# The second transposition of x ahead of two norms is issued one weight unit later on TensorE

## The chip, the cores and the metric

One core of one Trainium2 chip runs the whole program in one launch. The metric is the device time of that launch in microseconds (us). All data is float32; matrix operands are split into an upper part (rounded to the format that TensorE reads in one pass) and a lower part (what is left), and every product is built from upper x upper, lower x upper and upper x lower.

## The reference, cut to what matters

The program is a stack of two transformer blocks over 256 tokens of width 1024. The part around the change is the end of the first block's mixer, its feed-forward block, and the feed-forward block that opens the second:

```
x = x + rmsnorm(mixed @ w_out, norm_mix_post)         # ends with x new, "n = 1"
h = rmsnorm(x, norm_ffn_pre)                          # norm n1
f = (silu(h @ ffn_w_gate) * (h @ ffn_w_up)) @ ffn_w_down
x = x + rmsnorm(f, norm_ffn_post)                     # x new again, "n = 2"
h = rmsnorm_2(x, ffn1_norm)                           # norm n2
x = x + 0.5 * swiglu(h, ffn1_w_gate, ffn1_w_up, ffn1_w_down)
...
k, v = split(rmsnorm_2(mem, mem_kv_norm) @ w_kv)      # norm n4, depends on the input mem alone
```

The row factor of a norm (one over the root of the mean square) is applied after the products, so the products need only x times the norm's weights, turned so that features lie on partitions.

## The kernel before

**Weights as units.** All weights stream through 358 units of up to 128 x 1024 numbers. For unit u, SyncE fetches it into one of four `raw` buffers, ScalarE makes the upper part `whi` (L1419), VectorE the lower part `wlo` (L1807), and TensorE multiplies. This pair of operations is called the split of u. A fetch of u + 4 is issued once the split of u is done; the upper part of u waits until TensorE has used u - 4.

**One order for all engines.** `order()` writes out one list of steps: "split u", "unit" (the multiplication), "end" of a product (its results leave the PSUM banks), "do" (a named piece of work) and "step" (the next piece of a spawned task). Each engine runs through the same list, in order, and issues the part that is its own. A split stands two units ahead of its multiplication (`AHEAD = 2`).

**Around the change.** There are two places.

- Place A. The product `mkv0` (a quarter of the memory's keys and values, four units 73 to 76 of 24 matmuls 128 x 256 each) does not need x. It covers the making of n1. Units 77 and 78 are the first gate/up chunk `f0gu0`, 79 and 80 the second, `f0gu1`, each unit with 8 matmuls of 512 columns and 8 of 256. Unit 77 needs features 0 to 3 (of eight groups of 128) of the turned x, unit 78 features 4 to 7.
- Place B. `mkv1` (units 143 to 146) stands in the same way ahead of n2, but is followed by `mkv2` (units 147 to 150) and `mkv3`, each unit with 12 matmuls of 512 columns. These need n4 and not x; the first gate/up unit is 155.

`new1_0` and `new1_1` are the two halves of the turning for n1, `new2_0` and `new2_1` those for n2. The list holds, for place A before the change:

```
unit 75 | split 78 | do new1_1 | unit 76 | end mkv0 | split 79 | unit 77 | step rest1 | split 80 | unit 78 | ...
```

Of `new1_1` TensorE issues eight transposes of x (L1022, `half` and `turned`) into two small PSUM banks. ScalarE issues two pairs of activations that write the upper part of the turned x with the norm's weights (L1437, L1438), and behind them the four squares with sums over x (L1459) that the norm's row factor needs. VectorE issues the four operations that write the lower part (L1822); the last of each pair says that a bank is free and the two features are ready. GpSimd and SyncE have no part in it.

Behind these stand, on ScalarE: the upper parts of 79 and 80. On VectorE: `end mkv0` (two operations, L1894, which wait for unit 76), the lower part of 79, then the first step of the task `rest1`: it adds the sums of squares (L1857), waits for two GpSimd operations (the power -0.5), polishes the root with four small operations (L1845 to L1851) and makes two diagonal matrices (L1865). Behind that stands the lower part of 80. The task's TensorE part (`across`, L1037) comes after unit 80. Place B is the same with 149 and 150 for 79 and 80, and `mkv1` for `mkv0`.

Of the kernel before, what the change touches and what calls it, by code (L numbers as in the profile page):

```python
# [310 lines left out]
def order(chunks, n_units):  # L311
# [4 lines left out]
    def split_to(u):  # L316
        while split[0] <= min(u, n_units - 1):
            yield "split", None, 0, split[0]
            split[0] += 1

    def tick():
        for name in list(left):
            yield "step", name, 0, 0
            left[name] -= 1
            n, ahead = THEN.get(name, (None, 0))
            if n and left[name] == ahead:
                spawn(n)
            if not left[name]:
                del left[name]
# [6 lines left out]
    def spawn(name):  # L336
        left[name] = STEPS[name]

    def do(name):
        yield "do", name, 0, 0  # L340

    def product(name, mid={}, end_first=False, ahead=0, open_end=False, lead=AHEAD):
        for j, u in enumerate(chunks[name]):
            yield from split_to(u + lead)
            if j in mid:
                yield from mid[j]()
            yield "unit", name, j, u
            if end_first and u == chunks[name][-1]:
                yield "end", name, 0, 0
            yield from tick()  # L350
            if u == chunks[name][-1]:
                yield from split_to(u + ahead)
        if not end_first and not open_end:
            yield "end", name, 0, 0
# [69 lines left out]
    yield from woven(("wo0", "wo1"), ahead=AHEAD + 1)  # L424
    yield from drain()
    yield from do("sum0")
    yield from product("mkv0", {2: lambda: do("new1_0"), 3: lambda: do("new1_1")})
    spawn("rest1")
    yield from ffn(0)
    yield from do("row2")  # L430
    yield from product("f0dn0", {10: drain})
    yield from product("f0dn1", ahead=AHEAD + 1)
    yield from do("sum1")
    yield from product("mkv1", {2: lambda: do("new2_0"), 3: lambda: do("new2_1")})
    spawn("rest2")
    for n in (2, 3):
        yield from product(f"mkv{n}")
# [52 lines left out]
def build(nc, io):  # L490
    with ExitStack() as ctx:
# [247 lines left out]

        units, chunks, _ = unit_plan()  # L740
        plan = list(order(chunks, len(units)))
        ends = {name: chunks[name][-1] for name in chunks}
        loaded = {u: PRODUCTS[name][0] != "a" for name in chunks for u in chunks[name]}
# [2122 lines left out]
```

## Time and profile before

| | us |
|---|---|
| median of 3 runs (1051.99 to 1052.07) | 1052.0 |
| the profiled execution's own time | 1052.19 |
| its span, first to last instruction | 1050.3 |
| TensorE (PE) busy in the span | 1040.3 |
| VectorE (DVE) busy | 773.3 |
| ScalarE (ACT) busy | 601.8 |
| GpSimd (POOL) busy | 30.7 |
| mean granted TensorE clock | 0.998 |

The profile names PE for TensorE's matmuls, PEld for its weight loads, DVE for VectorE, ACT for ScalarE, POOL for GpSimd and SPq for the queue of fetches. A matmul's duration holds its way through the array, so matmuls overlap, and the start of one to the start of the next says how long each keeps the engine. On DVE and ACT, too, an operation may start up to 0.1 us ahead of the shown end of the one before.

### The profile page before, as it was taken

How to read it: one execution, taken by the hardware profiler on the slowest of the kernel's cores; microseconds unless marked ns; L12 is line 12 of the kernel's file. 1: busy time of each engine (PE TensorE's matmuls, PEld its weight loads, DVE VectorE, ACT ScalarE, POOL GpSimd, SP SyncE). 2: the span in 40 equal slices, each digit the busy share in tenths (PEclk: the TensorE clock that was granted, in tenths of full speed). 3: DMA queues.
4: the chain of work that ended last, by engine and by line, in shares of the span. 5: the costliest groups of instructions: out<-in, count | busy, mean ns of one | idle time of the engine just before them, and what ended most of it. 6: DMA issues, size and time to landing. Idle time of an engine off the chain costs nothing.

```text
span 1050.3 us, 16507 instructions
## 1 busy us (share of the span) xinstructions
PE 1040.3 (99%) x6496; PEld 935.6 (89%) x6496; DVE 773.3 (74%) x1301; ACT 601.8 (57%) x986; POOL 30.7 (3%) x45
## 2 busy tenths in 40 slices
PE   9999999999999999999999999999999999999997
PEld 8898888899999889899898899898888999999986
DVE  5796775988888855678787555868778668888854
ACT  6653675566555644555555446546756557555653
POOL 0000500010000000000000000100000000000000
PEclk9999999999999999999999999999999999999999
DMA  8755647556666666677787568533465445666662
GB/s 287 252 176 168 200 161 250 190 180 206 196 203 203 235 193 188 213 258 217 242 284 225 172 208 316 197 120 128 136 243 182 156 142 202 199 202 199 217 197 87
DMA packets 63896, 210.91 MB, mean 201 GB/s; under 512 B 7531, under 2 KB 14883, under 8 KB 62924
## 3 DMA queue, kind: packets, MB, share of 16 engines
q1 hardware_dynamic: 63676, 209.61, 60.9%
q8 instruction: 51, 0.84, 0.3%
q10 hardware_dynamic: 144, 0.26, 0.1%
q14 instruction: 25, 0.20, 0.1%
HBM read 206.41 MB, written 5.27 MB: 202 GB/s over the span
## 4 chain that ended last, share of the span: by engine, by line
PE 93%; DVE 2%; issue 2%; ACT 1%; DMA 0%; POOL 0%; SPq 0%; POOLq 0%; DVEq 0%; ACTq 0%
PE ps L975 22%; PE ps L958 14%; PE ps L959 14%; PE ps L960 14%; PE ps L977 11%; PE ps L966 3%; PE ps L968 3%; PE ps L969 3%; PE ps L1022 1%; PE ps L1158 1%; PE ps L1144 1%; PE ps L1071 1%; PE ps L1302 1%; DVE wlo_b L1807 0%; DMA m_kvx<-m_kvs 0%
## 5 line engine op out<-in xcount | busy, mean ns | idle before, releaser
L975 PE MATMUL ps<-hT,whi_b 128*128 128x512 f32 x1056 | 346.8, 382 | 0.0
L977 PE MATMUL ps<-hT,wlo_b 128*128 128x256 f32 x1056 | 287.8, 273 | 0.0
L1807 DVE TENSOR_TENSOR wlo<-raw,whi 128x1024 fp32r<-128x1024 f32 (+1 forms) x178 | 216.4, 1228 | 79.0 <-ACT whi L1419 78.3
L1419 ACT ACTIVATE whi<-raw 128x1024 fp32r<-128x1024 f32 (+1 forms) x178 | 183.1, 1044 | 106.4 <-PE ps L960 79.2
L1807 DVE TENSOR_TENSOR wlo_b<-raw,whi_b 128x1024 fp32r<-128x1024 f32 (+2 forms) x182 | 219.4, 1210 | 25.5 <-ACT whi_b L1419 24.9
L975 PEld LDWEIGHTS ps<-hT,whi_b 128*128 128x128 f32 x1056 | 199.6, 189 | 29.0 <-issue 1.3
L1419 ACT ACTIVATE whi_b<-raw 128x1024 fp32r<-128x1024 f32 (+2 forms) x182 | 187.2, 1037 | 27.7 <-PE ps L960 12.8
L977 PEld LDWEIGHTS ps<-hT,wlo_b 128*128 128x128 f32 x1056 | 202.7, 192 | 0.0
L1508 ACT ACTIVATE f_small_part<-ps 128x512 f32<-128x512 f32 x66 | 39.6, 600 | 139.8 <-PE ps L977 139.8
L958 PE MATMUL ps<-whi,f_hid_hi 128*128 128x512 f32 x256 | 97.1, 379 | 0.0
L959 PE MATMUL ps<-wlo,f_hid_hi 128*128 128x512 f32 x256 | 97.0, 379 | 0.0
L960 PE MATMUL ps<-whi,f_hid_lo 128*128 128x512 f32 x256 | 97.0, 379 | 0.0
L958 PE MATMUL ps<-whi,hT 128*128 128x512 f32 (+1 forms) x248 | 95.4, 385 | 0.4 <-DVE wlo L1807 0.4
L959 PE MATMUL ps<-wlo,hT 128*128 128x512 f32 (+1 forms) x248 | 92.3, 372 | 0.0
L960 PE MATMUL ps<-whi,hT 128*128 128x512 f32 (+1 forms) x248 | 92.3, 372 | 0.0
L966 PE MATMUL ps<-hT,whi_b 128*128 128x256 f32 x304 | 84.9, 279 | 0.1
L969 PE MATMUL ps<-hT,whi_b 128*128 128x256 f32 x304 | 83.6, 275 | 0.0
L968 PE MATMUL ps<-hT,wlo_b 128*128 128x256 f32 x304 | 83.6, 275 | 0.0
L1987 DVE TENSOR_TENSOR f_sg<-ps,f_small_part 128x256 f32<-128x256 f32 x66 | 32.0, 484 | 58.4 <-ACT f_small_part L1508 58.4
L966 PEld LDWEIGHTS ps<-hT,whi_b 128*128 128x128 f32 x304 | 58.3, 192 | 2.4 <-issue 1.5
L968 PEld LDWEIGHTS ps<-hT,wlo_b 128*128 128x128 f32 x304 | 58.3, 192 | 0.1
L969 PEld LDWEIGHTS ps<-hT,whi_b 128*128 128x128 f32 x304 | 58.4, 192 | 0.0
(396 smaller groups left out, 1628.0 us busy)
## 6 DMA issues: line engine op xcount, KB each, us to landing
raw<-in_wflat SPq DMA_DIRECT2D x355, 512.0 KB, 4.2
wide<-scratch SPq DMA_DIRECT2D x4, 512.0 KB, 6.2
m_w<-in_cmp_k_w SPq DMA_DIRECT2D x4, 512.0 KB, 6.3
m_w<-in_cmp_v_w SPq DMA_DIRECT2D x4, 512.0 KB, 6.8
m_alibi<-in_c_alibi SPq DMA_DIRECT2D x1, 1536.0 KB, 9.3
x<-in_x SPq DMA_DIRECT2D x2, 512.0 KB, 7.3
m_memT<-in_memT SPq DMA_DIRECT2D x1, 1024.0 KB, 7.3
m_memx<-in_mem SPq DMA_DIRECT2D x1, 1024.0 KB, 9.5
```

What stands on the lines that cost most here:

```text
L958: e.matmul(o, xh, in_turn(hi[:, k, :]), start=first and k == 0, stop=False)
L959: e.matmul(o, xh, in_turn(lo[:, k, :]), start=False, stop=False)
L960: r = e.matmul(o, xl, in_turn(hi[:, k, :]), start=False, stop=last and k == kt - 1)
L966: e.matmul(o, hi[:, k, c], in_turn(xs.h(k0 + k)), start=first and k == 0 and f % 2 == 0, stop=False, skip_group_check=True)
L968: e.matmul(o, lo[:, k, c], in_turn(xs.h(k0 + k)), start=False, stop=False, skip_group_check=True)
L969: r = e.matmul(o, hi[:, k, c], in_turn(xs.l(k0 + k)), start=False, stop=last and k == kt - 1, skip_group_check=True)
L975: e.matmul(o[:, :], hi[:, k, c], xs.hl(k0 + k), start=first and k == 0, stop=False, skip_group_check=True)
L977: r = e.matmul(o[:, 0:256], lo[:, k, c], in_turn(xs.h(k0 + k)), start=False, stop=last and k == kt - 1, skip_group_check=True)
L1419: e.activation(slot(whi, u)[:, w], raw[u % NRAW][:, w], ACT.Copy).then_inc(*w_hi.did(u, c))
L1508: e.activation(small_part[:, :, :], psum[:, b:b + 2, 256:512], ACT.Copy).then_inc(*hid_s.did(i, c))
L1807: e.tensor_tensor(slot(wlo, u)[:, w], raw[u % NRAW][:, w], slot(whi, u)[:, w].bitcast(F32), ALU.subtract).then_inc(*w_lo.did(u, c))
L1987: e.tensor_tensor(o, ps.tile(name, j)[:, 0:256].rearrange("p (b a) -> p a b", a=2), small_part[:, j, :].rearrange("p (b a) -> p a b", a=2) ...
```

## The change

In both places the second half's turning is taken out of the middle of the product and put behind its last unit, ahead of the product's "end". `open_end=True` makes `product` leave out its own "end", which is written out by hand behind the moved step.

```diff
-    yield from product("mkv0", {2: lambda: do("new1_0"), 3: lambda: do("new1_1")})
+    yield from product("mkv0", {2: lambda: do("new1_0")}, open_end=True)
+    yield from do("new1_1")
+    yield "end", "mkv0", 0, 0
     spawn("rest1")
     yield from ffn(0)
...
-    yield from product("mkv1", {2: lambda: do("new2_0"), 3: lambda: do("new2_1")})
+    yield from product("mkv1", {2: lambda: do("new2_0")}, open_end=True)
+    yield from do("new2_1")
+    yield "end", "mkv1", 0, 0
     spawn("rest2")
```

The list now reads, for place A: `unit 75 | split 78 | unit 76 | do new1_1 | end mkv0 | split 79 | unit 77 | ...`.

## Rows read from the trace of the kernel before

**Rows 1.** The page: busy time and share of each engine.

```profile
PE 1040.3 (99%) x6496; PEld 935.6 (89%) x6496; DVE 773.3 (74%) x1301; ACT 601.8 (57%) x986; POOL 30.7 (3%) x45
```

**Rows 2.** Timeline of PE, place A: start, duration, engine, line, operands.

```profile
236.22 1.04 PE L1022 MATMUL ps<-cst,x 128*128 128x128 f32 x8
237.01 0.36 PE L966 MATMUL ps<-m_n_hi,whi_b 128*128 128x256 f32 x1
237.21 0.28 PE L968 MATMUL ps<-m_n_hi,wlo_b 128*128 128x256 f32 x1
...
239.78 0.38 PE L975 MATMUL ps<-hT,whi_b 128*128 128x512 f32 x1
...
242.40 0.38 PE L975 MATMUL ps<-hT,whi_b 128*128 128x512 f32 x1
...
245.02 0.38 PE L975 MATMUL ps<-hT,whi_b 128*128 128x512 f32 x1
...
247.64 0.38 PE L975 MATMUL ps<-hT,whi_b 128*128 128x512 f32 x1
```

**Rows 3.** Timeline of ACT, place A; in brackets idle time and its releaser.

```profile
237.08 0.47 ACT L1437 ACTIVATE hT<-ps,cols 128x256 fp32r<-128x256 f32 x1 [1.03 <-PE ps L1022]
...
241.51 2.00 ACT L1419 ACTIVATE whi_b<-raw 128x1024 fp32r<-128x1024 f32 x2
```

**Rows 4.** Timeline of DVE, place A.

```profile
239.21 1.65 DVE L1822 SCALAR_TENSOR_TENSOR hT<-ps,cols,hT 128x256 fp32r<-128x256 f32 x4
240.78 1.27 DVE L1894 TENSOR_TENSOR m_ckT<-ps,rT 128x512 f32<-128x512 f32 x2
242.59 1.23 DVE L1807 TENSOR_TENSOR wlo_b<-raw,whi_b 128x1024 fp32r<-128x1024 f32 x1 [0.54 <-ACT whi_b L1419]
...
244.98 0.16 DVE L1845 TENSOR_TENSOR sm<-sm,stat 128x2 f32<-128x2 f32 x1 [1.09 <-POOL stat L2542]
...
246.17 1.22 DVE L1807 TENSOR_TENSOR wlo_b<-raw,whi_b 128x1024 fp32r<-128x1024 f32 x1
```

**Rows 5.** Timeline of ACT and DVE where a turned half found DVE idle.

```profile
624.41 0.47 ACT L1437 ACTIVATE hT<-ps,cols 128x256 fp32r<-128x256 f32 x1 [2.27 <-PE ps L1022]
...
625.28 1.66 DVE L1822 SCALAR_TENSOR_TENSOR hT<-ps,cols,hT 128x256 fp32r<-128x256 f32 x4 [0.53 <-ACT hT L1438]
```

**Rows 6.** Timeline near the start, where PE waited for a split.

```profile
24.79 1.22 DVE L1807 TENSOR_TENSOR wlo<-raw,whi 128x1024 fp32r<-128x1024 f32 x1
...
26.06 0.48 PE L958 MATMUL ps<-whi,hT 128*128 128x512 f32 x1 [0.42 <-DVE wlo L1807]
```

**Rows 7.** Timeline of PE, place B.

```profile
422.44 0.36 PE L966 MATMUL ps<-m_n_hi,whi_b 128*128 128x256 f32 x1
...
430.38 0.38 PE L958 MATMUL ps<-whi,m_n_hi 128*128 128x512 f32 x1
...
432.98 0.38 PE L958 MATMUL ps<-whi,m_n_hi 128*128 128x512 f32 x1
```

**Rows 8.** Timeline of ACT and DVE, place B.

```profile
426.94 2.94 ACT L1419 ACTIVATE whi<-raw 128x1024 fp32r<-128x1024 f32 x3
...
428.01 1.23 DVE L1807 TENSOR_TENSOR wlo<-raw,whi 128x1024 fp32r<-128x1024 f32 x1 [0.52 <-ACT whi L1419]
...
431.60 3.49 DVE L1807 TENSOR_TENSOR wlo<-raw,whi 128x1024 fp32r<-128x1024 f32 x3
```

**Rows 9.** Operations of line L2542: least, median, longest duration in ns.

```profile
L2542 POOL TENSOR_TENSOR stat<-sm,expo x7: 694/697/1574, 22.8 to 876.8; 128x2 f32<-128x2 f32 x7
```

**Rows 10.** The page's DMA issues: KB each, median us to landing.

```profile
raw<-in_wflat SPq DMA_DIRECT2D x355, 512.0 KB, 4.2
```

**Rows 11.** Stretches at the end: PE, PEld, DVE, ACT, POOL busy; then PEclk.

```profile
1043.00:1044.00 1.00, 0.76 (x7) 0.57 (x6) 0.75 (x3) 0.48 (x2) 0.00 (x0) 1.00 0.00 0
...
1046.00:1047.00 1.00, 0.00 (x0) 0.00 (x0) 0.91 (x2) 0.72 (x1) 0.00 (x0) 1.00 0.26 106
1047.00:1048.00 1.00, 0.00 (x0) 0.00 (x0) 0.00 (x0) 0.00 (x0) 0.00 (x0) 0.54 1.00 393
```

## The prediction

> **What bounds the kernel now.** I read the page first: PE is busy in 99% of the span, DVE in 74%, ACT in 57% [rows 1]. So the time is the sum of what TensorE issues plus the few moments in which it waits, and there are only two questions: does the change alter TensorE's own work, and does it make TensorE wait? The second is answered by the timelines of PE, ACT and DVE around the two places. What the reader should see in PE's timeline is that units follow each other without a gap: 77 starts at 239.78, 78 at 242.40, 79 at 245.02, 80 at 247.64, each 2.62 us after the one before [rows 2]. DVE's timeline shows how narrowly this succeeds. The lower part of unit 80 starts at 246.17 and takes 1.22, so it is ready at 247.39. A signal from DVE reaches PE in about 0.05: near the start a split ran from 24.79 for 1.22, to 26.01, and the waiting matmul started at 26.06 [rows 6]. With 0.06 (both stamps are rounded) unit 80 is ready at 247.45 and used at 247.64, a margin of 0.19 us [rows 2, 4]. Unit 79 is ready at 242.59 + 1.23 + 0.06 = 243.88 and used at 245.02, a margin of 1.14. Place B looks the same: the lower part of 149 is ready at 428.01 + 1.23 + 0.06 = 429.30 against its use at 430.38 (margin 1.08), and that of 150 at 431.60 + 1.22 + 0.06 = 432.88 against 432.98, a margin of 0.10 [rows 7, 8].
>
> **What is removed and added.** Nothing. The same eight transposes, activations, squares and subtractions are issued in each place. On TensorE the transposes take 0.79 us from their first start to the next unit's [rows 2], before and after. They do not wait for x in the place where they stand now (no idle time at 236.22 [rows 2]), so a later place saves no wait. The first matmul behind them takes 0.20 to its successor, 237.01 to 237.21, and the other 23 of unit 76 take (239.78 - 237.21) / 23 = 0.112 [rows 2]. That extra 0.08 or 0.09 moves along with the transposes to unit 77 and 147: sum 0.
>
> **What is moved.** In the written order only TensorE's part passes something, namely unit 76 (in place B, 146). For ACT and DVE "split 78, new1_1, split 79" is the same sequence as before, since units are TensorE's alone. GpSimd and SyncE have no part in the moved step, so it passes nothing in their queues. But both ACT and DVE must now wait longer for the transposed x. The delay is unit 76 without the switch: 24 x 0.112 = 2.68 us. The transposes then start at 236.22 + 2.68 = 238.90.
>
> **What queues behind it on ACT.** The first activation started 0.86 after the first transpose (236.22 to 237.08 [rows 2, 3]), with idle time in front of it, so ACT was already bound to this event. It now starts at 239.76. From it to the upper part of unit 79 there is a chain without a gap: four activations, four squares with their sums, then `whi` at 241.51 [rows 3]. 4.43 us of work, all of it in the queue ahead of the split. So the upper part of 79 starts at 241.51 + 2.68 = 244.19, 2.68 later than before. ACT has no earlier work left to fill the gap with: it idled 1.03 there before [rows 3] and now idles 3.71.
>
> **What queues behind it on DVE.** The lower part of the turned half begins when the upper part of two features is there. At 624.41 the same activations met an idle DVE, whose subtractions started 0.87 after them and lasted 1.66 [rows 5]. Here that gives 239.76 + 0.87 = 240.63 to 242.29, and 242.35 at TensorE, against unit 78's start at 242.40 [rows 2]. So the nearest consumer of the second half is just covered, by 0.05, and even a miss there would cost nothing extra as long as a later wait is longer. Then the two operations of `end mkv0` (1.27 [rows 4]) end by 243.5, and DVE waits for the upper part of 79. Before, DVE waited for it too (0.54 of idle time, ended by ACT [rows 4]), so the whole delay of 2.68 passes through: lower part of 79 at 245.27, ready at 246.56. Behind it stand the sum of squares, the GpSimd wait (1.09 [rows 4]), the polish and the diagonal, and then the lower part of 80. Nothing in this piece waited for anything but itself and GpSimd, so it moves as one: 246.17 + 2.68 = 248.85, ready at 250.13.
>
> **What TensorE then loses, place A.** Unit 79 waits from 245.02 to 246.56, 1.54 us. It takes 2.62, to 249.18. Unit 80 is ready at 250.13: another 0.95. Together 2.49 us, which is 2.68 - 0.19, the delay less the margin of unit 80. The two waits do not add beyond that, as the later ready time decides.
>
> **Place B.** The three upper parts from 426.94, 2.68 later, start at 429.62 (ACT's idle time in front of the turned half is of the same kind as in A; I take the same delay). The lower part of 149 was bound to ACT as well (0.52 idle [rows 8]). Unit 149 is ready at 431.98 against 430.38: 1.60. It takes 2.60 (430.38 to 432.98 [rows 7]), to 434.58; unit 150 is ready at 432.88 + 2.68 = 435.56: 0.98. Sum 2.58 = 2.68 - 0.10. That x is only wanted at unit 155 here does not help: what is late is the weights' split behind the squares, not x.
>
> **Is it given back?** TensorE has no slack to give [rows 1]. The next splits are not late: in A the lower part of 81 follows 80 after the two evictions of `f0gu0`, about 250.07 + 0.8 + 1.2 = 252.1 (an estimate: two operations of no more than L1822's pace, 1.65 for four, and a split [rows 4]), while unit 80 itself lasts until 250.13 + 2.62 = 252.75. Later fetches: that of unit 83 waits for the split of 79 (246.5) and lands 4.2 later [rows 10], near 250.7; its split is due after unit 80, so it lies beneath. No term.
>
> **The sum.** 2.49 + 2.58 = 5.07 us. Against the profiled execution's own time that is 1052.19 + 5.07 = 1057.26 (the span 1050.3 + 5.07 = 1055.4, with 1.89 outside it). The median of the runs stands 0.19 below the profiled execution: 1057.07. Forecast **1057.1**.
>
> **Bounds of its terms.** The delay is at least 24 x 0.111 = 2.66 and at most the whole stretch of 2.77 from 237.01 to 239.78: -0.04 to +0.18 for both places. Each margin may be off by 0.1, as it comes from rounded stamps and ends that overlap: 0.2 both ways. The GpSimd power in the chain mostly takes 0.70, but once took 1.57 [rows 9]; if a shifted start meets that, one place is dearer by 0.87. Likeliest case's own range: 1056.7 to 1057.6.
>
> **Rivals.**
> 1. *The lead hides it* (not slower). One mechanism: the splits stand two units ahead, and the only consumer of the second half, unit 78, is covered by 0.05. For: unit 79 alone has 1.1 us of margin. It decides if the splits of 80 and 150 are late by less than their margins of 0.19 and 0.10, which needs ACT to reach the split without the squares and the turned half ahead of it. Against: ACT idled in front of the turned half and DVE in front of the split, so no buffer lies between. Time 1052.0. Chance 4%.
> 2. *One place only.* In B the chain has some reserve that the rows hide, or the delay in A is swallowed. Time 1052.0 + 2.5 = 1054.5 (in A alone) or 1054.6. Chance 4%.
> 3. *The clock falls.* Two idle stretches of 1.5 and 1.0 us, 2.6 apart, might cost TensorE its clock. At the end of the trace PE's last matmul ran in 1043 to 1044; 1046 to 1047 was still granted 1.00, and only 1047 to 1048 shows 0.54, half of 2.4 GHz for most of it [rows 11]. So TensorE stood idle there for longer than either of these waits, and the clock was still full. If it fell all the same for one unit's length, that unit would take 2.62 more, at each place: 1057.1 + 5.2 = 1062.3. Chance 3%.
> 4. *GpSimd's power meets its long case once* [rows 9]: 1057.1 + 0.9 = 1058.0. Chance 5%.
> A gain has no place to come from: no wait is removed, and TensorE's work is the same.
>
> The Trainium skill, "TensorE: Matmul & The Clock Gate", section "HAM oscillation — how this bites in real kernels", says that waits between bursts of matmuls throw the clock back to its lower level, and speaks against any change that adds them. It is the rule of rival 3; the trace agrees that idleness lowers the clock, at 1047, but not that a short wait does.
>
> **How the numbers follow.** Forecast 84%, rivals 4, 4, 3 and 5%. About 0.2% (2.1 us) is what a measurement of this kernel can tell from no change. Slower by more than that are the forecast and rivals 2, 3, 4: 95%, with 1% off for what I did not see. Same is rival 1: 4%. The range leaves out rivals 1 to 3 and takes in rival 4 and twice the bounds of the terms, since both margins are small differences of large numbers: 1056.1 to 1058.3.
>
> **What the changed kernel's profile would show.** PE at place A: unit 76's 24 matmuls directly behind unit 75, transposes at about 238.9, no gap at 242.40; an idle time of 1.5 before the first matmul of unit 79 and 1.0 before that of 80, released by DVE L1807. ACT idle 3.7 before L1437 in place of 1.03. In place B 1.6 and 1.0 before L958. PEclk 1.00 throughout. TensorE's busy time unchanged. I am wrong if PE shows no idle time behind L1807, if the idle time in front of unit 80 is missing while that of 79 is there (then DVE's queue is more elastic than I think, and the loss is 1.5 a place), or if later waits shrink by what these two add.

## The result, and the profile after

| | kernel before | changed kernel |
|---|---|---|
| median of 4 runs, us | 1052.02 (1051.99 to 1052.07) | 1057.39 (1056.97 to 1058.24) |
| profiled execution: its time, its span | 1052.19, 1050.3 | 1056.97, 1055.1 |
| TensorE busy | 1040.3 | 1041.1 |

The ratio of the changed kernel to the one before is 1.0051, 95% interval 1.004 to 1.0063: slower by 5.4 us. 1057.1 was forecast. Of the executions compared below two were slow ones, one of the kernel before (4677 us) and one of its variant with fewer squares (6230 us), and every ratio leaves them out.

The page of the changed kernel answers to [rows 1]:

```profile
PE 1041.1 (99%) x6496; PEld 935.7 (89%) x6496; DVE 773.6 (73%) x1301; ACT 601.5 (57%) x986; POOL 30.5 (3%) x45
```

The same 6496 matmuls, 1301 VectorE and 986 ScalarE operations, with busy times within 1 us of before: nothing was added. The view of waits on PE (engine, line, who was waited for: us in total, times, longest) shows where the time went:

```profile
PE ps L962 <- DVE wlo L1811: 2.6, 3, 1.4
PE ps L979 <- DVE wlo_b L1811: 2.0, 2, 1.4
```

The changed kernel's lines stand four lower than before: L1811 is the lower part of the weights (L1807 before), L979 the gate/up matmul (L975), L962 the first matmul of a unit such as 147 (L958). The two rows are five waits for a split. One of them, 0.4 us, stands near the start in both kernels [rows 6]; the other four are new. The timeline of PE in place A, against [rows 2]:

```profile
238.53 1.04 PE L1026 MATMUL ps<-cst,x 128*128 128x128 f32 x8
239.32 0.46 PE L979 MATMUL ps<-hT,whi_b 128*128 128x512 f32 x1
...
242.02 0.45 PE L979 MATMUL ps<-hT,whi_b 128*128 128x512 f32 x1
...
246.26 0.45 PE L979 MATMUL ps<-hT,whi_b 128*128 128x512 f32 x1 [1.38 <-DVE wlo_b L1811]
...
249.74 0.48 PE L979 MATMUL ps<-hT,whi_b 128*128 128x512 f32 x1 [0.62 <-DVE wlo_b L1811]
...
252.46 0.61 PE L1041 MATMUL ps<-diag,ones 128*128 128x128 f32 x4
```

The reader is to see that unit 78, the consumer of the moved half, starts at 242.02 with no wait listed (by how little is told below, under "Unit 78"), and that 79 and 80, whose weights are merely queued behind that half, each wait. (In this execution everything ahead of place A was 0.37 us earlier than in the profile before, so distances between rows are to be compared, not times.) The queues of ScalarE and of VectorE, against [rows 3] and [rows 4]:

```profile
239.38 0.47 ACT L1441 ACTIVATE hT<-ps,cols 128x256 fp32r<-128x256 f32 x1 [3.71 <-PE ps L1026]
...
243.81 1.99 ACT L1423 ACTIVATE whi_b<-raw 128x1024 fp32r<-128x1024 f32 x2
```

```profile
240.26 1.66 DVE L1826 SCALAR_TENSOR_TENSOR hT<-ps,cols,hT 128x256 fp32r<-128x256 f32 x4 [1.34 <-ACT hT L1442]
...
244.89 1.23 DVE L1811 TENSOR_TENSOR wlo_b<-raw,whi_b 128x1024 fp32r<-128x1024 f32 x1 [1.77 <-ACT whi_b L1423]
...
247.28 0.16 DVE L1849 TENSOR_TENSOR sm<-sm,stat 128x2 f32<-128x2 f32 x1 [1.09 <-POOL stat L2546]
...
248.47 1.22 DVE L1811 TENSOR_TENSOR wlo_b<-raw,whi_b 128x1024 fp32r<-128x1024 f32 x1
```

ScalarE idles 3.71 in front of the turned half (1.03 before). From there to the upper part of 79 it takes 243.81 - 239.38 = 4.43 us, and 4.43 before (241.51 - 237.08 [rows 3]): an unbroken queue that moved as one piece. VectorE waits for it (1.77, against 0.54 before). From the lower part of 79 to that of 80 it is 248.47 - 244.89 = 3.58, and 3.58 before [rows 4].

Place B, PE, against [rows 7]:

```profile
426.53 1.04 PE L1026 MATMUL ps<-cst,x 128*128 128x128 f32 x8
...
434.17 0.48 PE L962 MATMUL ps<-whi,m_n_hi 128*128 128x512 f32 x1 [1.42 <-DVE wlo L1811]
...
437.74 0.48 PE L962 MATMUL ps<-whi,m_n_hi 128*128 128x512 f32 x1 [0.71 <-DVE wlo L1811]
```

How much each place costs can be read between two fixed points of TensorE's order, the first of the eight transposes and the first matmul of `across` (L1041 after, L1037 before). Without a wait, in place A, these would be 250.26 - 236.22 - 2.68 = 11.36 us apart once unit 76 is no longer between them (before, the timeline shows L1037 at 250.26); they are 252.46 - 238.53 = 13.93 apart. Place A costs 2.57. In place B the same (before: transposes at 421.65, L1037 at 435.56; after: 426.53 and 440.44) gives 13.91 against 11.23: 2.68. Together 5.25 us, against the 5.37 between the medians. The span of this one execution is only 4.8 us longer, because it was 0.37 ahead at place A and gained about 0.1 behind place B.

The clock, in place A (stretch; PE, PEld, DVE, ACT, POOL busy; PEclk; DMA share and rate):

```profile
244.00:248.00 4.00, 2.62 (x17) 2.19 (x16) 1.92 (x6) 4.00 (x5) 0.89 (x2) 1.00 0.18 33
```

TensorE was idle for 1.4 of 4 us and the granted clock stayed at 1.00, as it did in the four us that follow, which hold the wait of unit 80. In place B, from 432 to 436, it was idle for the same 1.4 us at 1.00.

### The profile page after: what moved, and what is told of

It is laid out like the page before. It is cut to its first block, busy times and chain, and to the rows that moved or that the text cites. A ratio compares the mean times of both kernels' runs of the same rounds, so it can differ in the third digit from the quotient of the medians.

```text
span 1055.1 us, 16507 instructions
## 1 busy us (share of the span) xinstructions
PE 1041.1 (99%) x6496; PEld 935.7 (89%) x6496; DVE 773.6 (73%) x1301; ACT 601.5 (57%) x986; POOL 30.5 (3%) x45
## 4 chain that ended last, share of the span: by engine, by line
PE 92%; DVE 3%; issue 3%; ACT 2%; POOL 0%; ACTq 0%; POOLq 0%; DVEq 0%
PE ps L979 21%; PE ps L962 14%; PE ps L964 14%; PE ps L963 14%; PE ps L981 11%; PE ps L970 3%; PE ps L973 3%; PE ps L972 3%; PE ps L1026 1%; PE ps L1162 1%; PE ps L1148 1%; PE ps L1075 1%; PE ps L1306 1%; DVE wlo_b L1811 1%; ACT junk L1463 0%
## 5 line engine op out<-in xcount | busy, mean ns | idle before, releaser
L979 PE MATMUL ps<-hT,whi_b 128*128 128x512 f32 x1056 | 347.2, 383 | 2.0 <-DVE wlo_b L1811 2.0
L1811 DVE TENSOR_TENSOR wlo<-raw,whi 128x1024 fp32r<-128x1024 f32 (+1 forms) x178 | 216.3, 1227 | 80.1 <-ACT whi L1423 79.4
L1811 DVE TENSOR_TENSOR wlo_b<-raw,whi_b 128x1024 fp32r<-128x1024 f32 (+2 forms) x182 | 219.7, 1212 | 26.6 <-ACT whi_b L1423 26.2
L979 PEld LDWEIGHTS ps<-hT,whi_b 128*128 128x128 f32 x1056 | 199.6, 189 | 31.4 <-issue 2.9
L962 PE MATMUL ps<-whi,f_hid_hi 128*128 128x512 f32 x256 | 97.1, 379 | 0.0
L962 PE MATMUL ps<-whi,hT 128*128 128x512 f32 (+1 forms) x248 | 95.4, 385 | 0.4 <-DVE wlo L1811 0.4
```

The source lines that it names most:

```text
L962: e.matmul(o, xh, in_turn(hi[:, k, :]), start=first and k == 0, stop=False)
L979: e.matmul(o[:, :], hi[:, k, c], xs.hl(k0 + k), start=first and k == 0, stop=False, skip_group_check=True)
L1811: e.tensor_tensor(slot(wlo, u)[:, w], raw[u % NRAW][:, w], slot(whi, u)[:, w].bitcast(F32), ALU.subtract).then_inc(*w_lo.did(u, c))
```

## The experiments

Times are medians; each kernel was compared with the kernel before on the same chip. "Cost of a place" is the distance between the two fixed points above, less that without a wait. Two theories stood against each other throughout. The first is the prediction's: what costs is the split of weights queued behind the late half. Rival 1 here (not that of the prediction) is the more natural reading: x reaches its consumer too late.

### One place at a time

The kernel before, with one of the two hunks of the diff each.

```diff
-    yield from product("mkv0", {2: lambda: do("new1_0"), 3: lambda: do("new1_1")})
+    yield from product("mkv0", {2: lambda: do("new1_0")}, open_end=True)
+    yield from do("new1_1")
+    yield "end", "mkv0", 0, 0
```

> The kernel before with the change in place A alone (mkv0). Theory (the weights' splits queue behind the late turned half): TensorE waits at units 79 and 80 as in the changed kernel, 2.57 us in all, so about 1054.6 us against 1052.0. Rival 1 (what counts is x reaching its consumer, unit 78, in place A only): the whole 5.2 us come from here, 1057.2 us. Nothing changes at units 149 and 150.

> The kernel before with the change in place B alone (mkv1), where x is wanted only eight units after its turning. Theory: TensorE waits at units 149 and 150, 2.67 us in all, about 1054.7 us. Rival 1 (late x is what costs): nothing, 1052.0 us, as x is there long before unit 155.

Place A alone: 1054.63 us against 1052.04 (ratio 1.0025, 1.0016 to 1.0034), and in its trace 13.93 us between the fixed points, 2.57 of them cost: as expected. Its place B is 13.92 long, against 13.91 before. Place B alone: 1055.49 (ratio 1.0032, 1.002 to 1.0044), of five runs of which two were at 1054.6 and three between 1055.5 and 1056.5; the median is 0.8 over what was expected. Its profiled execution was the longest of these, but the cost of place B in it is 13.90 - 11.23 = 2.67; the excess lies elsewhere (see "The changed kernel again"). What follows: the two places are independent and cost alike, although x is wanted one unit after its turning in the one and eight units after in the other. Rival 1 falls with place B.

### Half the delay

Only TensorE's order differs from the kernel before: the transposes stand after 12 of the last unit's 24 matmuls.

```diff
                     for f in range(n // 128):
+                        if f == 2 and last and name in ("mkv0", "mkv1"):
+                            half(1 + int(name[3]), 1)
...
             def new(i, n):
-                half(i, n)
+                if n == 0:
+                    half(i, n)
```

> In both places the eight transposes of the second half stand in the middle of the product's last unit, after 12 of its 24 matmuls. Only TensorE's order differs from the kernel before. Theory: the delay is 12 x 0.112 = 1.34 us in place of 2.68, the loss is the delay less the margin of units 80 and 150 (0.19 and 0.10) plus about 0.1 for the restarted matmuls: 1.15 + 1.24 + 0.2 = 2.6 us, about 1054.6 us. Rival 2 (a loss for each interruption, through the clock or a restart, whatever its length): about as much as the changed kernel, 1057.2 us. If the two-unit lead hid a moderate delay: 1052.0 us.

1054.59 us against 1052.04 (ratio 1.0026, 1.0016 to 1.0036). The PE timeline lists one wait in place A and one in place B, each for the second split (unit 79 starts 0.27 late too, at 245.38 where 245.11 was due, which is too short for the view to list):

```profile
248.86 0.48 PE L977 MATMUL ps<-hT,whi_b 128*128 128x512 f32 x1 [0.62 <-DVE wlo_b L1810]
```

```profile
435.52 0.48 PE L958 MATMUL ps<-whi,m_n_hi 128*128 128x512 f32 x1 [0.71 <-DVE wlo L1810]
```

The cost is 1.23 in A and 1.34 in B, for a delay of 1.34. At 2.68 it was 2.57 and 2.68. So past the margin each further 1.34 us of delay costs 1.34 us. Rival 2, about as much as the changed kernel whatever the length, falls. A fixed price for each listed wait would still fit this run, as one wait in place of two costs half; it falls with the next experiments, in which a place with one listed wait costs 0.56, 0.66, 0.99 or 1.08. The theory had set the cost as delay less margin, plus a little for the restart; that the margins of 0.19 and 0.10 are just about used up by that little (cost = delay - 0.11 and delay - 0.00) is a matter of 0.1 us a place.

### The split put back in front, with x just as late

This is the cleanest separation of the two theories. TensorE's order is exactly that of the changed kernel; the number of splits in front of the moved turning grows by one and by two, in both places.

```diff
-    yield from product("mkv0", {2: lambda: do("new1_0")}, open_end=True)
+    yield from product("mkv0", {2: lambda: do("new1_0")}, open_end=True, ahead=AHEAD + 1)
```

> The changed kernel, but with the split of unit 79 (149 in place B) in front of the moved turning, in the queues of ScalarE and VectorE. TensorE's order is that of the changed kernel, so x is turned just as late. Theory: units 79 and 149 no longer wait. The lower part of 80 (150) still stands behind the squares, the sum and GpSimd, but no longer behind the upper part of 79: the sum can start at 244.2 in place of 246.4, and the loss falls to about 0.3 in A and 0.4 in B, with restarts 0.9 us: 1052.9 us. Rival 1 (late x costs): as the changed kernel, 1057.2 us.

1053.29 us against 1052.04 (ratio 1.0013, 1.0004 to 1.0022), where 1052.9 was expected. In the trace, places A and B cost 0.56 and 0.66, 1.22 together where 0.9 was expected; in A most of the difference is that the sum of squares could start only at 244.34 (L1861 below) and not at 244.2. Of DVE's timeline in place A:

```profile
238.04 2.35 DVE L1811 TENSOR_TENSOR wlo_b<-raw,whi_b 128x1024 fp32r<-128x1024 f32 x2
240.59 1.66 DVE L1826 SCALAR_TENSOR_TENSOR hT<-ps,cols,hT 128x256 fp32r<-128x256 f32 x4 [0.20 <-ACT hT L1442]
...
244.34 0.16 DVE L1861 TENSOR_TENSOR stat<-stat 128x2 f32<-128x2 f32 x1 [0.89 <-ACT junk L1463]
```

The time in which VectorE stood idle before is now used for the split of 79 (the second of the x2 at 238.04), and what is left of the delay comes through the squares (0.89 of waiting for them) to the split of 80. Three quarters of the loss are gone with x turned as late as in the changed kernel.

> The changed kernel, but with the splits of units 79 and 80 (149 and 150) in front of the moved turning in the queues of ScalarE and VectorE. Theory: no split waits behind the squares any more, so place B loses nothing. In place A the subtractions of the turned half now stand behind the lower part of 80, which waits for unit 76: they end near 242.9, and unit 78, due at 242.40, waits about 0.5 us: +0.6 us in all, 1052.6 us. Rival 1 (late x costs by itself): as the changed kernel, 1057.2 us.

1053.05 us against 1052.14 (ratio 1.0007, 0.9998 to 1.0016: by the times alone no clear difference; the trace shows it). Place B costs 0.01: nothing is left there. Place A costs 0.90, where 0.6 was expected. It is a wait of unit 78, now really for x. Its first matmul starts at 243.19, 0.83 later than was due. The view of waits ascribes that to nothing ("issue"), but the weight load that belongs to it names the subtractions of the turned half:

```profile
243.16 0.19 PEld L979 LDWEIGHTS ps<-hT,whi_b 128*128 128x128 f32 x1 [0.94 <-DVE hT L1826]
```

VectorE's timeline has them at 241.44 for 1.65, so they end at 243.09, where 242.9 was expected. They stood behind the split of 80, whose upper part started at 239.17 on ScalarE:

```profile
239.17 1.07 ACT L1423 ACTIVATE whi_b<-raw 128x1024 fp32r<-128x1024 f32 x1 [1.74 <-DMA raw<-in_wflat]
```

The view names its fetch, which I had not counted. But unit 76's last matmul ended at 239.03, and the upper part of 79 had started 0.03 behind the end of unit 75 (236.35, 236.38), so the fetch held it up by about 0.1 at most. The cover of unit 78 was thin (0.05 by the prediction), and here it is gone.

### Less work in front of the split

The changed kernel, and the kernel before, with the squares over x's second half left out in both places; the norms' factors then come from the first half alone.

```diff
                 if n:
-                    for n in range(2):
-                        for t in range(2):
-                            q.wait_ge(*x_at(i, n, t))
-                        squares(i, n)
+                    for t in range(2):
+                        q.wait_ge(*x_at(i, 0, t))
+                    squares(i, 0)
```

> The changed kernel with two of the four squares left out in each place: the sums of squares over the second half of x are not computed, and the norms' factors come from the first half alone. Theory: ScalarE's chain in front of the split of 79 is 1.53 us shorter, the rest is as late as in the changed kernel: about 1.0 us is lost in A, 1.1 in B, with restarts 2.3 us over the kernel before: 1054.3 us. Rival 1 (late x costs): the squares stand behind the turned half, so leaving them out changes nothing: 1057.2 us.

> The kernel before with the same two squares left out in each place (the norms' factors from the first half of x alone). Theory: before, no split made TensorE wait, so a shorter chain buys nothing: 1052.0 us.

In the changed kernel the time falls from 1057.36 (its own runs in the same batch) to 1054.09; against the kernel before the ratio is 1.0017 (1.0009 to 1.0026). The cost is 0.99 in A and 1.08 in B. 1054.3 was expected. In the kernel before the same change gives 1052.17 against 1052.14 (ratio 0.9997, 0.9987 to 1.0006): nothing. ScalarE's queue of the changed kernel shows it: it starts at the same kind of wait, and reaches the split after 2.84 us in place of 4.43:

```profile
239.70 0.47 ACT L1441 ACTIVATE hT<-ps,cols 128x256 fp32r<-128x256 f32 x1 [3.72 <-PE ps L1026]
...
242.54 1.99 ACT L1423 ACTIVATE whi_b<-raw 128x1024 fp32r<-128x1024 f32 x2
```

So 3.18 us of squares that lie behind the turned half, and which x's consumer does not read, are worth 3.27 us in the changed kernel (by the traces 5.25 - 0.99 - 1.08 = 3.18, just what the two queues are shorter by) and nothing in the one before. The work in the queue has its price only once the queue starts too late.

### The changed kernel again

> The changed kernel once more, beside the others, for its spread (1056.97 to 1058.24 in four runs). Theory: the two places lose 5.2 us in every run, about 1057.3 us; a run near 1058.2 has one more wait of about 0.9 us, which I expect where GpSimd's power takes 1.6 us in place of 0.7.

1057.36 us (1057.09 to 1058.95), ratio 1.0047 (1.0033 to 1.006). Its profiled execution was the 1058.95. Both places look as before (waits of 1.39 and 0.62, 1.42 and 0.71). GpSimd's power was 0.7 there: my explanation for the longer runs was wrong. The excess of this execution arises in the first 25 us. ScalarE's timeline in it, and below it in the changed kernel's first profile (1056.97 us):

```profile
19.15 0.63 ACT L1463 ACTIVATE junk<-x 128x512 f32<-128x512 f32 x1 [1.96 <-DMA x<-in_x]
```

```profile
17.19 0.64 ACT L1463 ACTIVATE junk<-x 128x512 f32<-128x512 f32 x1 [0.32 <-DMA x<-in_x]
```

ScalarE waited 1.64 us longer for the load of x, which had been issued only 0.11 later (9.66 against 9.55), and a split behind it made TensorE wait 1.27 at 23.78. Place A then begins 1.96 later (240.49 against 238.53), which is nearly all of the 1.98 between the two executions (some 0.3 of it was there before this wait). The profiled execution of place B alone has the same two waits (1.85 of ScalarE for x, 1.3 of TensorE), and reaches place A 1.66 later than the kernel before: that is its excess. Among the runs of the kernel before a few are longer as well (26 runs beside the first four experiments reach 1053.25, the others 1053.69); none of these was traced, so their cause is not shown.

## Why the prediction was right

**Its own work.** "Nothing is removed or added" and "the switch moves along: sum 0" hold: transposes to the next unit take 0.79 before and after (239.32 - 238.53).

**The delay.** 2.68 was set. ScalarE's idle time rose by 3.71 - 1.03 = 2.68.

**What it passes through.** The chain on ScalarE (4.43) and on VectorE between the two splits (3.58) are the same to 0.01 in both traces. The experiments show that this is the cause: taking the split out of that queue takes away 4.0 of 5.25 us in the traces (one split) or 4.3 (two), and shortening the queue by the squares takes away 3.2.

**Unit 78.** Said to be covered by 0.05. It started on time, but the cover was a little less than nothing. The subtractions end at 240.26 + 1.66 = 241.92; the weight load of its first matmul starts at 241.99, 0.03 ahead of the matmul, where in the kernel before it stands 0.11 ahead (242.29 and 242.40), and the matmul takes 0.29 to its successor (242.02 to 242.31) in place of 0.22. With the turning 1.34 earlier ("Half the delay") it takes 0.22 again. The prediction counted to the matmul and not to its weight load. As it said, such a miss costs nothing: the 0.07 lies beneath the wait of unit 79. When the turned half was made later still, behind the second split, unit 78 was 0.83 late.

**The waits.** Unit 79 was to wait 1.54, unit 80 0.95; the view shows 1.38 and 0.62, as it counts an idle time from the modelled end of the last matmul. By starts, unit 79 stands 246.26 - 242.02 = 4.24 behind unit 78 where it stood 2.62, which is 1.62 later; 80 stands 3.48 behind 79, 0.86 later. The sum from there is 2.48, against the 2.49 that was forecast: the second unit starts when its split is ready, whatever came between. What the sum lacked stands behind that start. After a wait the first matmul takes longer to its successor (246.26 to 246.55, 0.29 in place of 0.22; 249.74 to 250.06, 0.32). At unit 79 this is swallowed, since unit 80 has to wait anyway; at unit 80 it is paid, some 0.1, and with it the place costs 2.57. In place B it is the same 0.1: 2.58 was forecast, 2.68 is in the trace. The expectations of the experiments put this term in. 5.07 was forecast, 5.25 is in the trace, 5.37 between the medians; the last 0.12 is within what the runs of one kernel differ by.

**The rivals.** *The lead hides it*: it does not, as its margin was 0.19. *One place only*: refuted by both single-place kernels. *The clock falls*: PEclk 1.00 with 1.4 us of idleness in 4. *GpSimd's long case*: the row was read wrongly. Its 1.57 or 1.58 us stands at the same place in every trace (one of seven, 219 to 221 us), and no trace has it at another; the one longer run of the changed kernel that was traced has another cause. The rule of the Trainium skill that was weighed ("TensorE: Matmul & The Clock Gate", "HAM oscillation — how this bites in real kernels") speaks of waits long enough to lower the clock, which the prediction's words leave open; the trace agrees that these were not long enough, with PEclk at 1.00.

**Given back?** No. From the `across` matmuls of place A to the transposes of place B it is 426.53 - 252.46 = 174.07 us, and 421.65 - 250.26 = 171.39 before; the difference of 2.68 is unit 146, which now stands in front of the transposes.

## What to carry to other kernels

When a step is moved on one engine, look past its consumer to whatever is queued behind the *receiving* operations on the other engines: here the moved data arrived in time to within 0.07 us, and the weights of two later units, unrelated to it, did not. A lead counted in units is worth only the smallest margin behind the slowest queue (0.10 to 0.19 us here, with "two units" on paper), and the margin can be read off the timeline as last ready time against first use. Where a step must be late, put the independent work that is due soon ahead of it in the in-order queues; that alone gave back three quarters with one split, and four fifths with two.

## What was not expected of the hardware

The first matmul after a wait keeps the array 0.07 to 0.1 us longer than its successors of the same shape (0.29 and 0.32 against 0.22 between starts), at the full granted clock. Its weight load starts with it or 0.03 ahead of it (246.23 and 246.26), where those of the same shape behind it start 0.11 ahead; unit 78 shows the same with no wait listed. A signal from VectorE to TensorE took 0.05 before unit 80 (249.69 to 249.74), as the prediction took it, but 0.14 before unit 79 (246.12 to 246.26); the runs do not show why. And the landing of x moved between executions of the same program (ScalarE's wait for it 0.32 or 1.96 us), and the execution with the later landing took 1.98 us longer.
